# Two-block transformer on one core: three low-half subtractions of weight tiles moved from VectorE to GpSimd, ahead of the first attention

## What is computed

```python
def diff_attention(h, w_qkv, w_o, lq1, lk1, lq2, lk2, subln_g, lam_init, cos, sin):
    qkv = h @ w_qkv                                  # 256x1024 @ 1024x3072
    ...
        s = jnp.einsum('bqhcd,bkhcd->bhcqk', qi, k).astype(jnp.float32)
        p = jax.nn.softmax(s, axis=-1)
        w = (p[:, :, 0] - lam * p[:, :, 1]).astype(v.dtype)
        return jnp.einsum('bhqk,bkhe->bqhe', w, v)
    ...
    o = rmsnorm(o, subln_g) * (1.0 - lam_init)
    return o.reshape(B_, S, A_N_HEADS * 2 * A_HEAD_DIM) @ w_o     # 256x1024 @ 1024x1024
```

## Time and profile before

| | |
|---|---|
| median of 3 runs | 1042.89 us |
| profiled execution, its time | 1042.97 us |
| profiled execution, its span | 1041.2 us |
| TensorE busy | 993.8 us, 95% |
| VectorE busy | 729.5 us, 70% |
| ScalarE busy | 548.5 us, 53% |
| GpSimd busy | 66.5 us, 6% |
| low halves (L1130) | 312 times, 1223 ns each, 378.1 us |
| high halves (L625) | 312 times, 1059 ns each, 326.8 us |

### The profile page before, as it was taken

How to read it: one execution, slowest core, us unless ns; L and a number is a source line. 1 busy time by engine, 2 the same in 40 slices (tenths; PEclk the granted TensorE clock), 3 DMA queues, 4 the chain that set the end, 5 groups by cost and what they waited for, 6 DMA issues and landing times.

```text
span 1041.2 us, 12793 instructions
## 1 busy us (share of the span) xinstructions
PE 993.8 (95%) x4744; PEld 814.4 (78%) x4744; DVE 729.5 (70%) x1025; ACT 548.5 (53%) x893; POOL 66.5 (6%) x118
## 2 busy tenths in 40 slices
PE   2999799999999999999999999999999999999997
PEld 2787577888888787777888886888888778888785
DVE  4988888876778797887665446647753777777653
ACT  4456836544443485575444436575546375455441
POOL 2100222000000401010000002000000010000000
PEclk9999999999999999999999999999999999999999
DMA  9998166998889473449865563856444467565551
GB/s 340 357 343 312 43 203 222 357 310 281 285 270 363 171 237 127 133 125 308 266 203 192 181 190 103 270 164 205 128 140 142 127 189 231 172 187 187 162 182 41
DMA packets 126966, 219.86 MB, mean 211 GB/s; under 512 B 9235, under 2 KB 78088, under 8 KB 126904
## 3 DMA queue, kind: packets, MB, share of 16 engines
q1 hardware_dynamic: 125488, 216.05, 63.1%
q0 software_dynamic: 1088, 2.87, 0.9%
q10 hardware_dynamic: 328, 0.12, 0.0%
HBM read 217.96 MB, written 1.05 MB: 210 GB/s over the span
## 4 chain that ended last, share of the span: by engine, by line
PE 82%; DVE 8%; ACT 4%; DMA 2%; issue 2%; POOL 1%; SPq 0%; DVEq 0%; POOLq 0%; ACTq 0%
PE bank L1844 16%; PE bank L1846 16%; PE bank L1845 16%; PE bank L1859 5%; PE bank L1861 5%; PE bank L1860 5%; DVE w_lo L1130 3%; PE bank L1906 2%; PE bank L1908 2%; PE bank L1907 2%; PE bank L1964 1%; ACT w_hi L625 1%; DMA raw<-in_f_w_in 1%; DVE ada_acc L1160 1%; PE bank L1940 1%
## 5 line engine op out<-in xcount | busy, mean ns | idle before, releaser
L1130 DVE TENSOR_TENSOR w_lo<-raw,w_hi 128x1024 fp32r<-128x1024 f32 x312 | 378.1, 1223 | 221.2 <-ACT w_hi L625 220.7
L625 ACT ACTIVATE w_hi<-raw 128x1024 fp32r<-128x1024 f32 x312 | 326.8, 1059 | 333.2 <-PE bank L1846 183.9
L1844 PE MATMUL bank<-w_hi,h_hi 128*128 128x512 f32 x768 | 307.2, 400 | 3.7 <-DVE w_lo L1130 3.7
L1846 PE MATMUL bank<-w_hi,h_lo 128*128 128x512 f32 x768 | 300.5, 391 | 0.0
L1845 PE MATMUL bank<-w_lo,h_hi 128*128 128x512 f32 x768 | 299.8, 390 | 0.0
L1844 PEld LDWEIGHTS bank<-w_hi,h_hi 128*128 128x128 f32 x768 | 144.8, 189 | 34.3 <-issue 6.1
L1846 PEld LDWEIGHTS bank<-w_hi,h_lo 128*128 128x128 f32 x768 | 144.6, 188 | 31.1
L1845 PEld LDWEIGHTS bank<-w_lo,h_hi 128*128 128x128 f32 x768 | 144.9, 189 | 29.5 <-issue 1.0
L1859 PE MATMUL bank<-w_hi,u_hi 128*128 128x512 f32 x200 | 78.6, 393 | 0.8 <-ACT av L1077 0.8
L1861 PE MATMUL bank<-w_hi,u_lo 128*128 128x512 f32 x200 | 77.9, 389 | 0.0
L1860 PE MATMUL bank<-w_lo,u_hi 128*128 128x512 f32 x200 | 77.9, 389 | 0.0
(11 more groups left out here) (313 smaller groups left out, 1255.1 us busy)
## 6 DMA issues: line engine op xcount, KB each, us to landing
raw<-in_f_w_in SPq DMA_DIRECT2D x176, 256.0 KB
ada<-in_ada_w SPq DMA_DIRECT2D x86, 512.0 KB, 5.8
raw<-in_w_in SPq DMA_DIRECT2D x46, 512.0 KB
raw<-in_f_w_out SPq DMA_DIRECT2D x44, 512.0 KB
raw<-in_w_up SPq DMA_DIRECT2D x88, 256.0 KB
raw<-in_a_w_qkv SPq DMA_DIRECT2D x24, 512.0 KB
raw<-in_w_down SPq DMA_DIRECT2D x22, 512.0 KB
raw<-in_b_w_qkv SPq DMA_DIRECT2D x12, 512.0 KB
```

The source lines that it names most:

```text
L625: nc.scalar.activation(w_hi[:, m % SPL], raw[:, m % RAW], ACT.Copy).then_inc(hi_done, 1)
L1130: ve.tensor_tensor(w_lo[:, m % SPL], raw[:, m % RAW], w_hi[:, m % SPL].bitcast(F32), ALU.subtract).then_inc(lo_done, 1)
L1844: mm(o, hi, w_hi[:, s, k], start=(u == 0 and k == 0), stop=False)
L1846: last = mm(o, lo, w_hi[:, s, k], start=False, stop=(u == 3 and k == 1))
```

## The change

GpSimd makes the low halves of the tiles 26, 27 and 28, one behind the other, in its program ahead of the eight heads. Each waits for the tile's high half and for the low half of the tile before. VectorE leaves these three out, keeps the folds that stood behind them where they were, and waits before tile 29 until `lo_done` has reached 29.

```diff
+POOL_LOWS = (QKV_A + 26, QKV_A + 27, QKV_A + 28)
@@ gpsimd, after the seven small loads, before `for h in range(8)`
+            for m in POOL_LOWS:
+                pool.wait_ge(hi_done, m + 1)
+                pool.wait_ge(lo_done, m)
+                nc.gpsimd.tensor_tensor(w_lo[:, m % SPL], raw[:, m % RAW], w_hi[:, m % SPL].bitcast(F32),
+                                        ALU.subtract).then_inc(lo_done, 1)
@@ vector, low(m)
                 m = at(m, turn, LOOP)
+                if m in POOL_LOWS:
+                    fold_after(m)
+                    return
                 v_.wait_ge(hi_done, m + 1)
+                if m == POOL_LOWS[-1] + 1:
+                    v_.wait_ge(lo_done, m)
                 ve.tensor_tensor(w_lo[:, m % SPL], raw[:, m % RAW], w_hi[:, m % SPL].bitcast(F32),
                                  ALU.subtract).then_inc(lo_done, 1)
+                fold_after(m)
+
+            def fold_after(m):
+
                 if m in TAKE_AFTER:
```

## The result

The changed kernel takes 1047.25 us, median of 11 runs; the kernel before, run beside it, 1043.47 us, median of 11. The ratio is 1.0037 with a 95% interval of 1.0029 to 1.0044: 3.9 us slower (3.0 to 4.6). The forecast was 3.8 us more.

The account below looks back on a forecast made before the run. TensorE, busy 95% of the span, was taken as the bound. Removals 0, hold 3.8 us and clock 0 on 1042.97 gave 1046.8 us, said as 1046.7 because the median is 0.08 lower; range 1042.6 to 1049.0 us.

Parts of the forecast that it names:

- The three removals: VectorE's subtractions for tiles 26, 27 and 28, 1.13 us each, were each worth 0 because waits behind them absorb it.
- GpSimd takes 2.4 us for 1024 columns: Each moved subtraction on GpSimd, scaled at 2.2 ns a column; 2.5 us with the semaphore, 7.5 us for three.
- The rival of a slow GpSimd: GpSimd's three subtractions take 4 us each instead of 2.4; time 1048.6 to 1053 us, chance 0.13.
- Its reads hold VectorE back, for the whole length: In the first two heads, each GpSimd subtraction stops VectorE's two-input SBUF operations for 2.25 us.
- The first rival: No hold: GpSimd barely holds VectorE and the 1.33 us slack absorbs it; 1042.9 us, chance 0.17.
- the small gain: VectorE's freed time removes TensorE's 0.91 us wait at 153.74; 1042.0 us, chance 0.05.
- the four cases: Turn orders of GpSimd and VectorE around the first L1445, making the attention 2.9, 5.1, 3.8 or 2.2 us late.
- the third: Two GpSimd operations go ahead of the pair L1445 and the third holds back L1395: 3.8 us late, the case taken.
- The argument that GpSimd is passed over between two operations in a row: Taken from the 156.44 us subtraction pair, it spoke against GpSimd's third operation coming between the two L1445 (5.1 us late).
- L1395 behind the maxima: The small VectorE operation between maxima and exponentials is held by GpSimd's third operation, from 108.8 to 109.75 us.
- The clock: The low-clock stretch in the attention may shrink or grow as TensorE's gap grows; taken as 0, with 0.9 us both ways.
- TensorE's wait: The wait before its second transposes in the attention, ending at 108.71, grows from 2.5 to about 6 us.

Follow-up runs that it names:

- e1_no_ops: The change with GpSimd's three subtractions replaced by one-column memsets, so these low halves are not made: ratio 1.0004 to the kernel before, interval 30.48 us.
- e5_late: The kernel before with only tiles 27 and 28 moved to GpSimd, behind its work for the sixth head: ratio 0.9997 to the kernel before.
- e2_write_only: The change with each GpSimd subtraction replaced by memsets of the same tile, some 2.4 us together, writing without reading: ratio 1.0011 to the kernel before.
- e4_two_tiles: The change with only tiles 26 and 27 on GpSimd, 28 staying on VectorE: ratio 1.0021 to the kernel before, interval 33.80 us.
- e8: The kernel before with two idle matmuls in TensorE's gap ahead of head 1's transposes: ratio 1.0001 to the kernel before, interval 28.99 us.
- e9: The change with idle matmuls, three ahead of head 0's transposes, one ahead of head 1's: ratio 1.0030 to the kernel before, interval 32.41 us.

## Why the prediction was right

- *The three removals are worth nothing.* Right, each in the way described: e1_no_ops shows the wait ahead of the maxima grow from 0.20 to 1.34 us (1.33 predicted), and nothing gained behind the attention.
- *GpSimd takes 2.4 us for 1024 columns.* It took 2.35 alone and 2.38 in e5_late; the row of 128 columns scaled well, and the new output type left no gap to explain. The rival of a slow GpSimd (4 us each) is out; its lower edge of 1048.6 us doesn't follow from its own 6.1 us, which give 1049.0. Half of the 4497 ns that the Trainium skill (GPSIMD Engine Reference, section 3.1) gives for 2048 columns is 2.25 us as an estimate, 0.1 us under the trace.
- *Its reads hold VectorE back, for the whole length.* Right: 1.92 us on an operation of 0.22, and with writes alone (e2_write_only) no two-input operation is slower. The first rival, that nothing is held, is out. So is the small gain, as TensorE's wait of 0.91 us is 0.92 in the changed kernel.
- *Who goes first.* None of the four cases came as written; nearest is the third, with one turn otherwise: the tie at 104.5 went to the first L1461, and GpSimd's second operation came in between the two L1461, not ahead of them. That makes the maxima 2.6 us late where 2.9 were worked out. The argument that GpSimd is passed over between two operations in a row did not hold for this pair.
- *L1395 behind the maxima.* Held for 0.83 us (0.95 worked out); e4_two_tiles, without the third operation, has it at 0.17. The trace and e5_late's L1173 agree with what the Trainium skill (SBUF — State Buffer, section "Who interferes with whom") states of `tensor_scalar`, and the maxima L1408, which kept 1.28 us beside a reading GpSimd, with what it states of `tensor_reduce`.
- *The clock.* Mis-sized: I took 0 and kept 0.9 us both ways; it was 0.9 more in the interval, shown by e8 and e9. The hold was 3.4 where I said 3.8, so the two errors cancel in part: 4.3 us in the interval. The totals say 3.9 (3.0 to 4.6), which holds 3.8 and 4.3 alike. That 3.9 lies so near the 3.8 of the forecast is luck; the range and the mechanism are what was right.
- *TensorE's wait* was to grow from 2.5 to about 6 us in one place. It did not: the chain has a step that I had passed over. The transposes of head 0, which stand ahead of the scores of head 3, wait for L1461 as well:

```profile
108.92 1.01 PE L2089 MATMUL bank<-ident,wgt 128*128 128x128 f32 x4 [2.77 <-DVE wgt L1461]
109.86 2.08 PE L2047 MATMUL bank<-qkT 64*128 64x256 f32 x8
113.70 1.09 PE L2089 MATMUL bank<-ident,wgt 128*128 128x128 f32 x4 [1.76 <-ACT wgtT L830]
```

The standing still is split in two, 2.77 and 1.76 us, with the scores at half clock between. The scores at 109.86 took 2.08 us at half the clock, and that cost nothing, as VectorE was held until later; the transposes and the products with V from 113.70 on did cost.

## What to carry to other kernels

Before work is moved from VectorE to GpSimd to free VectorE, look at what VectorE does in the same microseconds: a subtraction of 2.35 us on GpSimd that read SBUF stopped even an operation on two numbers per partition for 1.92 us, most of its own length. So such work belongs beside VectorE's work in PSUM (the maxima kept their 1.28 us) or where VectorE waits anyway (e5_late), not at the head of a chain of small steps. Look also at what the freed engine waits for next: three operations of 1.13 us were worth nothing, as each stood ahead of a wait that goes back to TensorE. And where a chain makes TensorE stand still, count the clock as a term of its own: here 0.9 us of the interval, too little for the totals to show.

## What the runs showed that was not expected

The granted clock stayed at 0.50 from 109 to 119 us in the change and from 110 to 113 before. It fell within a microsecond or so of the end of TensorE's gap (108.71 before, 108.92 after; in e4_two_tiles ahead of that end), and in the change it stayed low through the second gap. With four instructions (1.98 us) of idle matmuls in the gap (e8) it stayed at 1.00. At VectorE's own boundaries GpSimd comes in at times (between the two L1461) and at times not (between the two L1130 of the earlier trace rows); what decides was not tried. VectorE's `tensor_scalar` with one SBUF tile as input, of which no row of the kernel before showed this, was held beside GpSimd's subtraction much as the two-input operations were (2.45 us instead of 0.75).
